# Decay exponents of a state-space scan: from triangular matmuls to 32-row products

## The reference, cut to what matters

```
a_cs = cumsum(dt * A)                         # within a chunk
decay[l, s] = exp(a_cs[l] - a_cs[s]), l >= s  # else 0
y_diag = ((C B^T) * decay) @ (x * dt)
states = B^T (x * dt * exp(a_cs[last] - a_cs))
y_off  = C prev_state * exp(a_cs)
```

## Time and profile before

| | |
|---|---|
| median of 3 runs | 3817.04 us |
| profiled execution | 3818.76 us |
| its span | 3817.0 us |
| TensorE busy | 3641.6 us (95%) |
| VectorE busy | 2273.0 us (60%) |
| ScalarE busy | 1725.2 us (45%) |
| GpSimd busy | 557.0 us (15%) |
| mean granted TensorE clock | 0.982 of full |

### The profile page before, as it was taken

One profiled execution on the slowest core, in us unless ns is written; L12 is line 12 of the kernel. 1 busy time (PEld: TensorE's weight loads), 2 busy tenths in 40 slices (PEclk: granted clock), 3 DMA queues, 4 the chain that ended last, 5 costly groups with the idle time before them and its releaser, 6 DMA issues.

```text
span 3817.0 us, 48755 instructions
## 1 busy us (share of the span) xinstructions
PE 3641.6 (95%) x20278; PEld 3052.0 (80%) x20278; DVE 2273.0 (60%) x2931; ACT 1725.2 (45%) x2342; POOL 557.0 (15%) x437
## 2 busy tenths in 40 slices
PE   8999989999998998999999989999999999989998
PEld 7778878888876777777777768978888888778998
DVE  4445354456676665655565663468889888843332
ACT  5333344431125655666766772144554554442132
POOL 0001032200000444400000000012222222210001
PEclk9999999999999999999999999999999999999999
DMA  3012023342212011011111124121111111153111
GB/s 109 23 40 89 26 86 107 109 154 89 109 47 89 24 33 39 12 55 28 34 36 28 34 80 144 34 89 34 45 45 39 55 51 44 34 203 118 45 36 70
DMA packets 227392, 244.87 MB, mean 64 GB/s; under 512 B 10007, under 2 KB 190180, under 8 KB 227172
## 3 DMA queue, kind: packets, MB, share of 16 engines
q1 hardware_dynamic: 222391, 224.92, 18.3%
q10 hardware_dynamic: 4781, 16.84, 1.2%
HBM read 191.40 MB, written 50.33 MB: 63 GB/s over the span
## 4 chain that ended last, share of the span: by engine, by line
PE 81%; DVE 9%; ACT 6%; issue 2%; DMA 1%; POOL 1%; SPq 0%; ACTq 0%; DVEq 0%; POOLq 0%
PE pd L211 65%; PE pq L211 13%; PE pd L366 2%; PE pq L366 1%; DVE t L3461 1%; DVE t L328 1%; DVE t L3469 1%; ACT t L3066 1%; ACT t L320 1%; DVE t L3906 0%; DVE t L2404 0%; DMA yc_scratch<-t 0%; DVE t L3156 0%; DMA ym_scratch<-t 0%; DVE t L3138 0%
## 5 line engine op out<-in xcount | busy, mean ns | idle before, releaser
L211 PE MATMUL pd<-t 128*128 128x512 f32 (+2 forms) x15104 | 2892.6, 352 | 50.1 <-DVE t L2596 8.5
L211 PEld LDWEIGHTS pd<-t 128*128 128x128 f32 x15104 | 2399.8, 191 | 483.5 <-issue 99.2
L211 PE MATMUL pq<-t 128*128 128x128 f32 (+5 forms) x3846 | 680.7, 336 | 62.4 <-DVE t L3942 16.6
L211 PEld LDWEIGHTS pq<-t 128*128 128x128 f32 (+2 forms) x3846 | 502.8, 181 | 186.4 <-issue 47.6
L320 ACT ACTIVATE t<-t 128x2048 fp32r<-128x2048 f32 (+3 forms) x133 | 212.7, 1599 | 634.4 <-PE pd L211 591.6
L328 DVE TENSOR_TENSOR t<-t 128x2048 fp32r<-128x2048 f32 (+3 forms) x133 | 257.5, 1936 | 177.0 <-ACT t L320 176.6
L1919 DVE TENSOR_TENSOR t<-pd,t 128x512 f32<-128x512 f32 x256 | 172.8, 689 | 103.1 <-PE pd L211 100.9
L2061 POOL TENSOR_TENSOR t<-t 128x2 f32<-128x2 f32 x8 | 10.4, 1306 | 1259.7 <-DVE t L3306 851.9
L3858 POOL TENSOR_TENSOR t<-t 128x512 f32<-128x512 f32 x56 | 97.0, 1731 | 594.3 <-ACT t L3802 317.0
L3189 DVE COPY t<-pd 128x512 f32<-128x512 f32 x64 | 44.2, 691 | 216.5 <-PE pd L366 216.5
L3469 DVE SCALAR_TENSOR_TENSOR t<-t 128x1024 f32<-128x1024 f32 x120 | 172.5, 1437 | 0.5
(11 more groups left out here) (337 smaller groups left out, 2998.9 us busy)
## 6 DMA issues: line engine op xcount, KB each, us to landing
t<-in_w_in_dram SPq DMA_DIRECT2D x97, 512.0 KB, 4.2
t<-in_w_out_dram SPq DMA_DIRECT2D x20, 1024.0 KB, 5.2
t<-in_w_in_dram SPq DMA_DIRECT2D x16, 1024.0 KB, 5.2
t<-in_w_mlp_dram SPq DMA_DIRECT2D x64, 256.0 KB, 3.5
u_scratch<-t SPq DMA_DIRECT2D x64, 256.0 KB, 3.4
t<-in_w_mlp_dram SPq DMA_DIRECT2D x16, 1024.0 KB, 5.0
t<-u_scratch SPq DMA_DIRECT2D x15, 1024.0 KB, 7.2
t<-in_x_dram SPq DMA_DIRECT2D x16, 512.0 KB, 8.2
```

Of the source, the lines that this page charges most:

```text
L211: ins = e.matmul(out, l, r, start=(first and j == 0), stop=(last and j == n - 1), skip_group_check=True)
```

## The change

The exponent of a pair of positions is now a difference of running sums, written as a matrix product of few rows. For each group and direction, 32 rows hold for each of four heads the running sum at l (high and low float32r parts), its negative with log(dt) added (high and low), and selectors of one and zero. A matmul of 32 rows and 512 columns then gives a_cs[l] - a_cs[s] + log dt[s] for four heads at once. Forward and backward go to two banks, `("seg", 0)` and `("seg", 1)`. VectorE joins them in PSUM with one predicated copy under the mask `below`; ScalarE's exp follows. As log(dt) is in the exponent, W and its product go away.

- Removed: the eight ScalarE multiplies a step, GpSimd's `weights`, VectorE's product with W, `Ust`, `Lst`, `ddt`.
- `front` of the chunk two ahead is issued at the end of a step (before: one ahead), also across the border of two groups; select and exp of the chunk one ahead are issued in the step before their use.
- The setup gains a Ln on ScalarE, ten small VectorE operations that fill `QT`, eight transposes, six ScalarE operations (`TT`, `LT`) and four 128x1024 VectorE operations (`RR`). Its weight in `weave` goes from 8 to 10. Exp of A moves ahead of the Ln.

```diff
+    def pe_ssm_front(e, i, n):
+        for d in range(2):
+            b = e.take(PB, "seg", d, i, n)
...
+            q = 32 * (3 - i if d else i)
+            mms(e, b[:, :], [(LT[d][q:q + 32, tile(n)], RR[q:q + 32, n, :, :].rearrange("p h t -> p (h t)"))]).then_inc(
+                *at.inc("pe", "seg", d, i, n))
...
-    def act_ssm_scaled(e, i, n):
-        for r, tri, h0 in (("Rf", Uinc, 4 * i), ("Rb", Linc, 16 + 4 * i)):
-            x = e.take(Er, r, i, n, hold=r == "Rf")
-            for j in range(4):
-                e.mul(x[:, j, :], tri[:, :], dA[:, n, h0 + j:h0 + j + 1]).then_inc(*at.inc("act", r, i, n))
+    def act_ssm_exp(e, i, n):
+        x = e.take(Er, "E", i, n)
+        e.wait_ge(*at["Esel", i, n])
+        e.activation(x[:, :, :], four(PB.of("seg", 0, i, n)), ACT.Exp).then_inc(
+            *at.inc("act", "L", i, n, free=("seg", 0, i, n)))
...
+    def dve_ssm_select(e, i, n):
+        e.wait_ge(*at["seg", 0, i, n])
+        e.wait_ge(*at["seg", 1, i, n])
+        e.copy_predicated(four(PB.of("seg", 0, i, n)), bc(below[:, :, :], q4), four(PB.of("seg", 1, i, n))).then_inc(
+            *at.inc("dve", "Esel", i, n, free=("seg", 1, i, n)))
...
             e.wait_ge(*at["L", i, n])
-            e.wait_ge(*at["W", i, n])
-            e.tensor_tensor(x[:, :, :], x[:, :, :], Wr.of("W", i, n)[:, :, :], MUL).then_inc(
-                *at.inc("dve", "LW", i, n, free=("W", i, n)))
...
+        for th in range(2):
+            b = e.take(PB, "rows", th)
+            e.wait_ge(*at["QT"])
+            transposed(e, b, [QT[:, th * 4 + j, :].bitcast(F32) for j in range(4)]).then_inc(*at.inc("pe", "rows", th))
...
+        for j in range(4):
+            e.tensor_scalar(RR[:, :, j, :], TT[:, :].rearrange("p (n l) -> p n l", n=8), KC[:, 8 + j:9 + j],
+                            KC[:, 4 + j:5 + j], MUL, ADD).then_inc(*at.inc("dve", "RR", j))
...
-        weave((first, 8), (dense(e, 0), 32))
+        weave((first, 10), (dense(e, 0), 32))
```

More of the change, by code:

```diff
@@ L2095, in program @@
     Acc = ring(ph, 2, [128, S])
-    Er = ring(ph, 6, [128, 4, 128])
+    Er = ring(ph, 3, [128, 4, 128])
     trs = sbt(ph, [128, 512])
     Xw = ring(ph, 1, [128, 2, 256])
-    Wr = ring(ph, 1, [128, 4, 128])
-    Uinc, Linc, Ust, Lst = (sbt(ph, [128, 128]) for _ in range(4))
+    Uinc, Linc = (sbt(ph, [128, 128]) for _ in range(2))
     St = [sbt(ph, [128, 512]) for _ in range(2)]
+    KC = sbt(ph, [128, 12])
+    below = sbt(ph, [128, 1, 128], I32)
+    LT = [sbt(ph, [128, S], F32R) for _ in range(2)]
+    RR = sbt(ph, [128, NT, 4, 128], F32R)
     ph.close()
@@ L2222, in act_ssm_steps @@
         yield
-        act_ssm_scaled(e, 0, 0)
-        yield
-        act_ssm_scaled(e, 0, 1)
+        e.wait_ge(*at["KC"])
+        for th in range(2):
+            e.wait_ge(*at["rows", th])
+            b = PB.of("rows", th)
+            e.copy(TT[:, half(th)], b).then_inc(*at.inc("act", "TT", th))
+            for d in range(2):
+                e.activation(LT[d][:, half(th)], b, ACT.Identity, scale=KC[:, 2 * d:2 * d + 1],
+                             bias=KC[:, 2 * d + 1:2 * d + 2]).then_inc(*at.inc("act", "LT", d, th))
+            at.also("act", ("rows", th))
     def dve_ssm_steps(e):
@@ L2422, in b_ready, with then @@
         return [("xs", 8 + g, 1), ("silu", 10 + g)]
+    def then(i, n):
+        return (i, n) if n < 8 else (i + 1, n - 8)
+    def pe_ssm_front(e, i, n):
+        for d in range(2):
+            b = e.take(PB, "seg", d, i, n)
+            for th in range(2):
+                e.wait_ge(*at["LT", d, th])
+            for j in range(4):
+                e.wait_ge(*at["RR", j])
+            q = 32 * (3 - i if d else i)
+            mms(e, b[:, :], [(LT[d][q:q + 32, tile(n)], RR[q:q + 32, n, :, :].rearrange("p h t -> p (h t)"))]).then_inc(
+                *at.inc("pe", "seg", d, i, n))
     def pe_ssm_scan(e, i):
         CT, CB, Bt = BC[i // 2]
[L2431 to L2437, removed]
         def states(n):
@@ L2474, in pe_ssm_scan @@
             yield
[L2475 to L2476 removed]
+            if then(i, n + 2)[0] < 4:
+                pe_ssm_front(e, *then(i, n + 2))
             yield
         values(7)
[L2480 to L2486 removed]
+    def act_ssm_exp(e, i, n):
[3 more added lines that the diff above has]
+            *at.inc("act", "L", i, n, free=("seg", 0, i, n)))
     def act_ssm_scan(e, i):
[L2489 to L2492 removed]
+        if i == 0:
+            act_ssm_exp(e, 0, 0)
+            act_ssm_exp(e, 0, 1)
         yield
         for n in range(8):
[L2496 removed]
             yield
[L2498 to L2501 removed]
+            if n and then(i, n + 1)[0] < 4:
+                act_ssm_exp(e, *then(i, n + 1))
             yield
@@ L2546, in pool_ssm_scan @@
                 moved(n + 2)
-            weights(n + 1)
             if n < 3:
@@ L2586, in dve_ssm_scan @@
                 ins.then_inc(*at.inc("dve", "St", i, n + 1, free=("st", i, n)))
+            if n and then(i, n + 1)[0] < 4:
+                dve_ssm_select(e, *then(i, n + 1))
             yield
-            x = Er.of("Rf", i, n)
+            x = Er.of("E", i, n)
             for th in range(2):
```

92 lines of the change are left out of this document (56 added, 36 removed).

## The result

The changed kernel takes 3800.8 us (median of 5 runs, 3789.71 to 3804.18) against 3817.04 us (5 runs beside it, 3815.24 to 3819.07). The ratio is 0.9952 with a 95% interval of 0.9936 to 0.9969: faster by half a percent, 16 us by the medians and 18 by the ratio, where 33 were forecast.

A forecast was written before the change was run, and what follows sets the result against it. TensorE, busy 95% of the span, was taken as the bound; 35.5 + 3 + 2.9 + 2.4 - 7 - 3 = 33.8 us off 3818.76 gave 3785.0, with the median 1.7 lower, stated as 3784; range 3768 to 3805.

The forecast's parts named there:

- Front: TensorE's exponent products in the scans: each front falls from 1.71 to 0.6 us, 32 fronts save 35.5 us.
- Copy in PSUM: VectorE's predicated copy takes 0.743 us, replacing the product with W: 24.0 us out, 23.8 in.
- Rival (b): VectorE becomes the bound in the scans because the predicated copy costs twice as much in PSUM: 3802 us, chance 0.08.
- GpSimd: 64 operations, 89.4 us, leave GpSimd: VectorE gets back 7 us on L2612 and as much elsewhere; TensorE 3 us.
- Waits that go: TensorE's waits in the scans: 2.9 us for ScalarE's multiplies and 2.4 us of group 3's final wait for G go.
- the 3 us for `moved`: TensorE's 6.3 us of waits for `moved`, queued behind `weights` on GpSimd: half goes, 3 us.
- New waits: TensorE in the scans waits 7 us more: 5.3 us in stretches of plain steps, 2 us for VectorE's other work.
- The bank ring: Four PSUM banks, a step now taking three: front of chunk n+3 waits for exp of n+2.
- rival (c): Slower: front waits for exp, behind a Silu and VectorE's convolution, 49 us of waits: 3833 us, chance 0.07.
- Setup: Setup ahead of the scans: reordered sums, QT's transposes and added operations lose 3 us, ends 0 and 8.
- Nothing else changed: Sign in the trace: the stage from 1190 to 1620 shorter by 34 us, the stages behind not moved.
- (a): Dear front on TensorE: no overlap, full price for each change of split, 1.2 us each: 3803 us, chance 0.08.

The follow-up runs named there:

- rows128: The changed kernel with both front products over all 128 rows instead of 32, so no change of the array's split: 3792.61 us.
- nosel: The changed kernel without VectorE's predicated copy, exp reading the forward bank alone, scaled by zero: 3791.33 us.
- before_f32r: The kernel before with its front's operands rounded to float32r, two passes a step for four, nothing else of the change: 3800.84 us.
- xw2: The changed kernel with two buffers for `moved` instead of one, and two for `Er` instead of three: 3789.38 us.
- front_f32: The changed kernel with its new front's operands read as plain F32, four passes: 3818.9 us.
- before_xw2: The kernel before with two buffers for `moved` instead of one and nothing else changed: 3818.99 us, ratio 1.0008.

## Why the prediction was right, and where its sum was off

- **Front, 0.6 us, saving 35.5.** Right: 0.44 us to the next work and 0.19 round it, a step of 3.24 for the forecast 3.2, 34.9 us in 32 such steps. The overlap was there, and the 0.35 us taken for the two changes of split measured 0.37 against rows128.
- **Copy in PSUM, 0.743.** Right, 0.689. Rival (b) is out by that, and nosel bounds what the copy is worth.
- **GpSimd, 3 us and 7 back to VectorE.** Under-sized. I counted 14 us back to VectorE, 7 on L2612 and as much again elsewhere; VectorE's busy time changes by 27 us with GpSimd's work, and the time by 14.5, half of it through the clock. L2612's mean, forecast near 0.5, is 0.468. I had halved the gain on that line, when nearly all of it came.
- **Waits that go, 2.9 and 2.4.** Right, both are gone, and so are the other waits for G. Of the 3 us for `moved` 1 went.
- **New waits, 7 us.** The exp line shows 6.9 + 2.5 = 9.4 us where I said 5 to 8. L2639, the state's addition, came on top: 8.4 us, where the kernel before had 3.2 (below), a row that the prediction left aside. In all, TensorE's idle time in the scans rose by 2.5 us instead of falling by 1.3. The bank ring is real, but not rival (c): that needed over 30 us. The row of the waits before the change:

```profile
PE pq L211 <- DVE t L2585: 3.2, 2, 2.5
```

- **Setup, 3 us.** It took 6.7, within the ends 0 and 8. The long idle time ahead of the cumulative sums is 9.5 us, as forecast. Counted from D, the projections behind QT's transposes start 3.7 us later (1227.47 - 1186.86 against 1225.90 - 1189.01), near the 3 forecast. The other 3.0 came after it: a 48-matmul stretch of 12.72 us for 11.16, behind the 2.4 us wait for QT (rows below, before and after), 0.6 us for a late Silu, and 0.6 us for the longer way from front over the copy to exp ahead of the first `states`.

```profile
1225.90 11.16 PE L211 MATMUL pd<-t 128*128 128x512 f32 x48
```

```profile
1227.47 12.72 PE L211 MATMUL pd<-t 128*128 128x512 f32 x48
```

- **Nothing else changed, or it would be wrong.** The forecast asked for 34 us in the stage and none outside. The stage gave 11.8 in the profiled pair, and 6 came outside it. That is scatter of the size that the other versions show. The means over all runs differ by 17 us, so the stage's 11.8 is as likely too low as the rest is too high. The forecast of 3784 itself was 17 us too low, inside its range mainly because the range was wide enough for rivals (a) and (b), and neither of them happened.
- **The step that failed: the clock in the scans.** The sum counted each wait at its length and the busy time at full clock, and so put the scans' loss to the lower level at no change. At full clock it came near: 29 us measured, for 33.8 less the 3.7 us more that the setup took. The lower level then took 12 us (good to 3) that no term held. I had this effect before me in the setup and counted it there, and nowhere in the scans. Rows 2 show 0.97 and 0.98, which I read as a property of the stage and not as something the change would move; they became 0.91 and 0.95.

The evidence for this step: the clock column of every version, before_f32r (11 us lost with none of the change's new waits and orders), and xw2 (9 us given back, 1.6 at full clock). Why the clock falls more stays open. The reason that I had in mind, less work in a step between the same pauses, is not shown: front_f32 has more work, less idle time and a loss as large, before_f32r has 15 us more idle time than the kernel before and a clock as high as front_f32's, and before_xw2 loses 5 us more with unchanged steps. Nor is it shown why a given pause starts such a stretch and another doesn't: the kernel before also had a pause of 1.94 us for `moved` at this place, and a clock of 0.91 behind it.

## What to carry to other kernels

When work is taken off TensorE at 95%, don't take its clock as given: a pause can cost its length and, behind it, slower matmuls. Here that took 12 of 29 us. Look at the granted clock of the windows round each pause before you trust a sum, and compare span x clock and span x (1 - clock) between versions. A wait of a few us that an extra buffer removes can be worth more than its length. In the kernel before the same edit gained nothing, as another engine was late just behind the wait: test it in the kernel where you want it. Unused work on GpSimd isn't free: test a kernel with it put back to see what taking it off VectorE's side was worth. And compare profiles outside the changed stage too: what differs there is the scatter with which the stage's own difference must be read.

## What the runs showed of the hardware

- Two 32-row products of 512 columns in different row quarters and banks ran side by side, 0.50 us for both. The way in and out cost 0.37 us and the overlap saved 0.20: with 128 rows and no change of split the step is 0.16 us shorter.
- The same 308 VectorE instructions took 216.7 us, and 243.8 with 76 us more of GpSimd work beside them; those that got longer had their inputs in SBUF, those with one in PSUM kept their time.
- 14 us without idle time ran at a granted clock of 0.61, behind three pauses of 1.1 to 1.9 us.
- How much a version lost to the lower level followed neither its idle time nor its work: front_f32 had 23.2 us of idle time in the scans and before_f32r 40.8, both at a clock of 0.94, and the kernel before had 25.7 at 0.96.
